# Two-layer hybrid encoder, one core: output projections moved into the blocks of the feed-forward and of the merge

## The reference

```python
def _swiglu(x, w_in, w_out):
    gate, up = jnp.split(x @ w_in, 2, axis=-1)
    return (jax.nn.silu(gate) * up) @ w_out
```

## Time and profile before

| | |
|---|---|
| median of 3 runs | 4042.57 us (4038.04 to 4055.39) |
| the profiled execution's own time | 4024.74 us |
| span in its trace | 4022.9 us |
| TensorE busy | 3580.9 us, 89% |
| VectorE, ScalarE, GpSimd busy | 37%, 26%, 26% |
| mean granted TensorE clock | 0.924 of full speed |
| transfers | 236.77 MB, 59 GB/s in the mean |

### The profile page before, as it was taken

One profiled execution on the slowest core, in us unless ns is written; L12 is line 12 of the kernel. 1 busy time (PEld: TensorE's weight loads), 2 busy tenths in 40 slices (PEclk: granted clock), 3 DMA queues, 4 the chain that ended last, 5 costly groups with the idle time before them and its releaser, 6 DMA issues. The chain is left out here.

```text
span 4022.9 us, 76222 instructions
## 1 busy us (share of the span) xinstructions
PE 3580.9 (89%) x32360; PEld 3364.9 (84%) x32360; DVE 1495.6 (37%) x2554; ACT 1060.5 (26%) x1798; POOL 1048.1 (26%) x544
## 2 busy tenths in 40 slices
PE   6998899888979898998889898988788789889988
PEld 6998898776768888998889898987667679889987
DVE  4441144445763122442044403434458522134411
ACT  2221252112453113221222223421135521122211
POOL 2443234110011212443324342431000212124432
PEclk9999899997988998999989998999889889979998
DMA  2332221001110321332223231210021113213332
GB/s 65 89 93 80 64 64 48 3 2 40 45 30 19 97 60 54 89 93 77 67 71 92 81 89 53 68 25 3 2 54 37 43 37 79 63 51 91 89 83 65
DMA packets 458281, 236.77 MB, mean 59 GB/s; under 512 B 14718, under 2 KB 456332, under 8 KB 458012
## 3 DMA queue, kind: packets, MB, share of 16 engines
q1 hardware_dynamic: 458012, 232.90, 21.0%
HBM read 230.50 MB, written 2.10 MB: 58 GB/s over the span
## 5 line engine op out<-in xcount | busy, mean ns | idle before, releaser
L137 PE MATMUL PS<-u_high,W_high 128*128 128x264 f32 x3328 | 964.2, 290 | 46.9 <-POOL W_low L659 24.2
L138 PE MATMUL PS<-u_low,W_high 128*128 128x264 f32 x3328 | 955.0, 287 | 0.0
L139 PE MATMUL PS<-u_high,W_low 128*128 128x264 f32 x3328 | 954.4, 287 | 0.0
L137 PEld LDWEIGHTS PS<-u_high,W_high 128*128 128x128 f32 x3328 | 638.7, 192 | 48.8 <-POOL W_low L659 24.4
L138 PEld LDWEIGHTS PS<-u_low,W_high 128*128 128x128 f32 x3328 | 639.9, 192 | 0.5
L139 PEld LDWEIGHTS PS<-u_high,W_low 128*128 128x128 f32 x3328 | 636.6, 191 | 0.0
L152 POOL TENSOR_TENSOR W_low<-W,W_high 128x1024 fp32r<-128x1024 f32 x176 | 420.6, 2391 | 779.2 <-ACT W_high L146 779.2
L137 PE MATMUL PS<-u_high,dW_high 128*128 128x264 f32 (+1 forms) x1536 | 467.2, 304 | 19.3 <-POOL dW_low L1377 7.9
L1377 POOL TENSOR_TENSOR dW_low<-dW,dW_high 128x512 fp32r<-128x512 f32 x128 | 207.8, 1631 | 948.4 <-ACT dW_high L1372 948.2
L137 PE MATMUL PS<-hidden_high,W_high 128*128 128x264 f32 x1408 | 402.7, 286 | 56.7 <-POOL W_low L573 56.7
L138 PE MATMUL PS<-u_low,dW_high 128*128 128x264 f32 (+1 forms) x1536 | 443.6, 289 | 0.0
(11 more groups left out here) (341 smaller groups left out, 5469.8 us busy)
## 6 DMA issues: line engine op xcount, KB each, us to landing
W<-in_ffn_w_in SPq DMA_DIRECT2D x176, 512.0 KB, 4.0
dW<-in_w_in SPq DMA_DIRECT2D x188, 256.0 KB, 2.9
W<-in_ffn_w_out SPq DMA_DIRECT2D x64, 704.0 KB, 4.7
W<-in_w_in SPq DMA_DIRECT2D x32, 512.0 KB, 5.6
W_branch<-in_w_branch SPq DMA_DIRECT2D x16, 768.0 KB, 5.1
W<-in_w_out SPq DMA_DIRECT2D x16, 512.0 KB, 4.1
xt<-in_x SPq DMA_DIRECT2D x4, 512.0 KB
out<-ot SPq DMA_DIRECT2D x4, 512.0 KB, 2.7
```

Of the source, the lines that this page charges most:

```text
L137: nc.tensor.matmul(dst, wh, xh, start=first, stop=False)
L138: nc.tensor.matmul(dst, wh, xl, start=False, stop=False)
L139: return nc.tensor.matmul(dst, wl, xh, start=False, stop=final)
```

## The change

`phase_ffn_in` and the `phase_out` behind it become one function `phase_ffn` with one block, and the `phase_out` behind the merge goes into `phase_merge`. The block's end, the `clear` and the block's start between them are gone, 6 times in a run, and the weights of the output go through the same `W` buffers as those of the input, in one numbering of units. In the feed-forward an output tile now has three units, of 8, 8 and 6 chunks (`PARTS`), 24 in place of 16, because the buffers hold 8. A class `Out` holds what `phase_out` did on ScalarE (`put`) and VectorE (`gains`, `add`). TensorE waits for the parts of the hidden state (`hidden_low`) or of the mixture (a new signal `mixture`) chunk by chunk. In the merge the last chunk of output tile 0 is issued behind the first seven of tile 1. The signals by name are now drawn from a pool that each phase uses anew, so that 34 semaphores serve where over 130 names had one each, and `clear` zeroes so many fewer.

```diff
         def S(name):
...
             if name not in named:
-                named[name] = sem(name)
+                if len(named) == len(signals):
+                    signals.append(sem(f"signal{len(signals)}"))
+                named[name] = signals[len(named)]
             return named[name]
...
+        class Out:
+            def gains(self, v):
+                nc.vector.tensor_scalar(self.gs[:], prm[:, self.gain:self.gain + KD], self.scale, None, ALU.mult
+                                        ).then_inc(S("gs"), 1)
+
+            def put(self, act, m, ready):
+                ps = PS[:, 2 * (m % 4):2 * (m % 4) + 2, 0:H2]
+                act.wait_ge(tile_done, ready)
+                if m == 0:
+                    act.wait_ge(S("gs"), 1)
+                if m >= 2:
+                    act.wait_ge(S("added"), max(1, m - 2))
+                nc.scalar.activation(halves(ssq[:, m % 2]), ps, ACT.Square).then_inc(S("out_squares"), 1)
+                nc.scalar.activation(halves(fo[:, m]), ps, ACT.Copy, scale=self.gs[:, m:m + 1]
+                                     ).then_inc(S("out_put"), 1)
...
+        def phase_ffn(hh, hl, l, which, pre, gain):
+                PARTS = ((0, 8), (8, 8), (16, 6))
+                units = len(PARTS) * KD
...
                     def _(sp):
...
+                        for u in range(units):
+                            (k0, nk), c = PARTS[u % 3], u // 3 * P
+                            sp.wait_ge(S("split"), 2 * KF + u + 1)
+                            sp.dma_start(W[:, u % 2, 0:nk], wo[:, k0:k0 + nk, c:c + P]).then_inc(landed[u % 2], 16)
...
                     def _(g):
...
+                        for u in range(units):
+                            low_part(g, 2 * KF + u, W, WH, WL, u % 2, PARTS[u % 3][1])
...
                         with pe.Fori(1, NI) as i:
                             for s in range(4):
                                 tile(i, s)
+                        for u in range(units):
+                            m, (k0, nk) = u // 3, PARTS[u % 3]
+                            pe.wait_ge(S("split"), 2 * KF + u + 3)
+                            if k0 == 0:
+                                if m < 4:
+                                    pe.wait_ge(dve_evac, 2 * KF + m + 1)
+                                else:
+                                    pe.wait_ge(S("out_put"), m - 3)
+                            for k in range(k0, k0 + nk):
+                                if m == 0 and k in (0, 8, 16, 20, 21):
+                                    pe.wait_ge(S("hidden_low"), {0: 8, 8: 16, 16: 20, 20: 21, 21: 22}[k])
...
-                        silu(NI - 1, 1)
+                        for u in range(units):
+                            high_part(act, 2 * KF + u, 16 * (KF + u // 2) + 16, W, WH, u % 2, PARTS[u % 3][1])
+                            if u == 0:
+                                silu(NI - 1, 1)
+                            if u >= 4 and u % 3 == 1:
+                                out.put(act, u // 3 - 1, 2 * KF + u + 1)
+                        out.put(act, KD - 1, 2 * KF + units + 2)
...
-        def phase_merge(gates, y_of, mh, ml, l, st):
+        def phase_merge(gates, y_of, mh, ml, l, gain, st):
...
-                    for n in range(NG):
+                    for n in range(NT):
                         if n >= 2:
                             sp.wait_ge(S("split"), n - 1)
+                        if n >= NG:
+                            c = (n - NG) * P
+                            sp.dma_start(W[:, n % 2], wo[:, :, c:c + P]).then_inc(landed[n % 2], 16)
+                            continue
...
                         for n in (2 * m, 2 * m + 1):
-                            if n + 2 < NG:
-                                high(n + 2)
+                            high(n + 2)
                             gate(n)
+                    for m in range(KD):
+                        if NG + m + 2 < NT:
+                            high(NG + m + 2)
+                        out.put(act, m, NG + m + 1)
...
+                    for m in range(KD):
+                        pe.wait_ge(S("split"), NG + m + 1)
...
+                        for k in range(KD - 1):
+                            if m == 0:
+                                pe.wait_ge(S("mixture"), k + 1)
+                            out_block(m, k)
+                        if m == 1:
+                            pe.wait_ge(S("mixture"), KD)
+                            out_block(0, KD - 1)
+                        if m:
+                            out_block(m, KD - 1)
```

More of the change, by code:

```diff
@@ L438, in _, with __init__, add @@
                     lead.vector(v)
-        def phase_ffn_in(hh, hl, l, which, pre):
+        class Out:
+            def __init__(self, st, gain, scale):
+                self.gs = sb(st, "gs", [P, KD])
+                self.gain, self.scale = gain, scale
+            def gains(self, v):
[11 more added lines that the diff above has]
+                                     ).then_inc(S("out_put"), 1)
+            def add(self, v):
+                for m in range(1, KD - 1):
+                    v.wait_ge(S("out_squares"), m + 1)
+                    if m > 1:
+                        v.wait_ge(S("added"), m - 1)
+                    nc.vector.tensor_tensor(ssq[:, 2], ssq[:, 2] if m > 1 else ssq[:, 0], ssq[:, m % 2], ALU.add
+                                            ).then_inc(S("added"), 1)
+        def phase_ffn(hh, hl, l, which, pre, gain):
             with ExitStack() as st:
@@ L447, in phase_ffn_in @@
                 wi = ffn_w_in[ds(l, 1), which].rearrange("a (k p) n -> p (a k) n", p=P)
+                wo = ffn_w_out[ds(l, 1), which].rearrange("a (k p) n -> p (a k) n", p=P)
                 NI = KF // 2
+                PARTS = ((0, 8), (8, 8), (16, 6))
+                units = len(PARTS) * KD
+                out = Out(st, gain, 0.5)
                 lead = Lead(st, [hid[:, 0], hid[:, 1]], pre, (4, 6), True)
@@ L548, in _ @@
                                 v.wait_ge(S("hidden_low"), 2 * i + j + 1)
+                        out.gains(v)
+                        out.add(v)
             clear()
[L551 to L623, removed]
@@ L640, in phase_merge @@
             NG = 2 * KD
+            NT = NG + KD
+            out = Out(st, gain, 1.0)
             with nc.Block() as block:
@@ L708, in _, with out_block @@
                             last.then_inc(S("projected"), 1)
+                    def out_block(m, k):
+                        for a in range(2):
+                            half = slice(a * H2, (a + 1) * H2)
+                            last = exact(PS[:, 2 * (m % 4) + a, 0:H2], WH[:, m % 2, k], WL[:, m % 2, k],
+                                         mh[:, k, half], ml[:, k, half], k == 0, k == KD - 1)
+                        if k == KD - 1:
+                            last.then_inc(tile_done, 1)
+                    for m in range(KD):
+                        pe.wait_ge(S("split"), NG + m + 1)
+                        if m < 2:
+                            pe.wait_ge(act_evac, NG - 1 + m)
+                        elif m < 4:
+                            pe.wait_ge(S("multiplied"), 3 * KD - 3 + m)
+                        else:
+                            pe.wait_ge(S("out_put"), m - 3)
+                        for k in range(KD - 1):
[7 more added lines that the diff above has]
+                            out_block(m, KD - 1)
                 @block.vector
```

22 lines of the change are left out of this document (15 added, 7 removed).

## The result

| | before | changed |
|---|---|---|
| median | 4043.47 us (4038.04 to 4055.39, 4 runs) | 3935.61 us (3920.09 to 3947.17, 4 runs) |
| profiled execution, own time | 4024.74 us | 3944.31 us |
| its span | 4022.9 us | 3942.5 us |
| TensorE busy, mean clock | 89%, 0.924 | 91%, 0.934 |

The ratio of the runs is 0.9758, with a 95% interval from 0.9729 to 0.9787: faster by 2.1 to 2.7%. The two medians by themselves stand at 0.9733, 107.9 us apart. Measured again later (11 and 6 runs), the pair gave 0.9774 (0.9743 to 0.9804; 4021.11 against 3934.18 us). The forecast was 3962 / 4042.6 = 0.980, just outside the first interval and inside the second. The median itself lies 6 us under the range that was given, while the profiled execution came out at 3944.31 us, where 3944.1 stood. How both can be is the question of the second half of the experiments.

A forecast was written before the change was run, and what follows sets the result against it. Bound: TensorE idle at each output phase's start, waiting for its weights, then restarting at low clock. Feed-forwards 62.3 us plus merges 18.3 us make 80.6 us; 4042.6 us less that gives 3962 us, range 3942 to 3984.

The forecast's parts named there:

- The four boundaries: Between input and output stage of the four feed-forwards: idle 56.7 us and slow restarts 6.6 us go, 63.3 us.
- I take the difference, 0.3 us, four times: Leaving the input loop, four feed-forwards: 1.35 us against 1.09 us without a loop, costed at 1.0 us in all.
- Rival A: Leaving the hardware loop costs a fetch of 3.6 us, four times with a restart: 20 us, time 3982; chance 0.10.
- The clockwork of the joined stream: First feed-forward output unit is converted beside the last input tile, 3.6 us against 5.8 us, so TensorE need not wait.
- The two merges: Between branch products and output: 23.5 us idle and 3.8 us restarts go, 9.0 us added, net 18.3 us.
- The new wait: Merge output tile 2: the postponed chunk delays freeing a weight buffer, so TensorE waits 2.9 us, in each layer.
- The slow restart: Behind the merge's wait at tile 2: matmuls at the low clock lose 1.6 us, bounds 0 and 1.9 us.
- The units of 8, 8, 6: Feed-forward output: a unit of 6 lasts 4.3 us, the conversion beside it 3.6 us; tight, costed at nothing.
- rival C: Conversion becomes the bound at units of 6 chunks: 32 waits of 2.3 us with restarts, 125 us, time 4087; chance 0.02.
- The turns of the block: Barrier and clear between phases, 1.09 us a turn: shorter clears were taken to gain nothing.
- rival B: Block turns get shorter with 34 signals and 17 clears, not 23: at most 18 us, time 3944; chance 0.08.
- carried over to the median: The sum of 80.6 us, made on the profiled execution, was subtracted from the median of 4042.6 us too.

The follow-up runs named there:

- the small units: The changed kernel with feed-forward output units of 8, 8, 3 and 3 chunks in place of 8, 8 and 6: 3985.58 us, ratio 0.9900 to the kernel before.
- executions with evened starts: The kernel before and the changed kernel, each with 24 extra matmuls on constants at the start of each feed-forward: 4013.59 us and 3920.65 us.

## Why the prediction was right, and where it was off

**The four boundaries.** Forecast 63.3 us, less 1.0 for leaving the loop. Measured 63.3 in the first pair of traces. The step "I take the difference, 0.3 us, four times" was wrong: TensorE leaves its loop with no gap. It was also misread, for in the same trace VectorE leaves the same loop in feed-forward 1 in less than the 1.09 us of a place without a loop:

```profile
1859.03 0.17 DVE L615 TENSOR_SCALAR gs<-prm 128x8 f32<-128x8 f32 x1 [1.06 <-PEq L157]
```

In the changed kernel 0.3 us show on ScalarE, behind feed-forward 0 alone and inside its slack. Rival A fell: nothing like its 3.6 us shows at the loop's end on any engine.

**The clockwork of the joined stream.** It holds as it was carried over from the loop: transfer 13 us ahead, conversion done 1.6 to 1.9 us before its use, the hidden chain at 5 us where 4.9 was reckoned.

**The two merges.** Forecast 27.3 - 9.0 = 18.3, measured 18.1. The new wait was put at 2.9 us and is 2.90, twice. The slow restart was taken as 1.6 from a wait of 2.01 us in another place; removing the postponement gave 4.75 us a layer, so with what lies beside it (a slower first matmul, two half-slow ones) it is 1.85, just under the upper bound of 1.9 that was named. That the postponement buys nothing was shown by taking it out.

**The units of 8, 8, 6.** Costed at nothing, and TensorE is busy for 118 of 118 us there. That the conversion decides once a unit is shorter than its chain was shown by the small units. They also answer rival C's price: it put a slow restart of 1.6 us behind each wait, and 28 waits of 1.6 us brought none.

**The turns of the block.** Costed at nothing; rival B counted 17 clears against 23, where the traces have 21 against 27, and the clears turned out 1.8 us shorter in all. 63.3 + 18.1 - 3.6 (the starts, 184.1 against 187.7) make 77.8 of the 80.4 us between the two spans. The other 2.6 us lie outside the stretches, and the clears can hold 1.8 of them. How well that fits is worth little: what lies outside the stretches is 2159.9 us in the kernel before and 3.0 us more, not less, in the run with the pool alone, and in the kernels with joined feed-forwards it wanders from 2154.4 to 2160.6 us.

**The median.** The lower bound given for the gain, 75 us, sums to 75.6 by its own terms. The step that failed is "carried over to the median": I took the profiled pair's difference for the medians', with nothing for the starts of the feed-forwards and for the exposed transfers. The profiled execution of the kernel before lay 18.7 us under the median of its runs, and that of the changed kernel 8.7 us over the median of its own; these 27.4 us are the whole distance between 80.4 and 107.9. The starts took 41.8 to 56.4 us each, by when the clock rises. The two profiles happened to have starts that sum up to nearly the same (184.1 and 187.7), so the forecast fit them to 0.2 us, which is luck at that precision. Medians of executions with evened starts differ by 92.9 us. By the spans it is 93.4, 12.8 beyond my sum. The rests hold 6.8 of these (69.1 against 62.3) and the starts 1.9; the merges take 0.8 back (17.5 against 18.3). The other 4.8 us lie outside the stretches: 1.8 can be the clears, and 3 us stay unexplained, within what this part of the span wanders by. Why the first pair's medians lay 108 us apart is explained by the scatter of both kernels only in its size; all but one of those executions have no traces.

## What to carry to other kernels

A barrier between two phases can cost more than its own microsecond: here 0.9 to 1.35 us of turn, but 12 to 16 us of idle TensorE, because the weight stream starts again from nothing, and 1.7 to 1.9 us more for the restart at half clock. In this kernel it went when both phases drew from one numbered stream through the same buffers. Reordering the consumer to wait less for one input can hold the buffer of another: reckon for each buffer when it is given back. And before trusting a difference of profiled spans, look for stretches that the edit doesn't touch and compare them too.

## What the runs showed of the hardware

VectorE's sum of squares, with both inputs in SBUF, took 707 to 709 ns in the kernel before and mostly 2.6 us in the changed one (36 instructions; min, median, max in ns), since it now falls beside GpSimd's subtraction:

```profile
L478 DVE TENSOR_TENSOR ssq<-ssq x36: 708/2604/2758, 366.3 to 3897.4; 128x528 f32<-128x528 f32 x36
```

34 of the 36 run beside a subtraction of GpSimd that began 0.2 to 0.5 us earlier, and end 0.6 us after it; the other two, with GpSimd idle, took 708 ns. GpSimd's subtraction kept its 2.40 us. The Trainium skill (SBUF — State Buffer, Who interferes with whom) has the one of the two that is issued later blocked until the first is done. The trace agrees: it is VectorE that loses 1.9 us, and nobody waits for it.

TensorE's granted clock outlasted waits of 1.6 us 28 times and fell after one of 2.90 us, but only nine matmuls later; and in the same code it rose in the first of eight steps or in the sixth. Matmuls on constants in waits that are there anyway were worth some 3 us for each feed-forward (24 of them, 11.4 us between the medians of the kernel before without and with them), and cut the scatter of its runs from 27 us to 10.

Clearing a range of semaphores took 0.07 us for the first two clears of the program text, whose ranges are short, and 0.29 us for the last ones, with some 160 semaphores in the range.
